# Up projection with both parts of x side by side as one 512-column operand, in 43 groups

## The chip, the cores and the metric

One core of a Trainium2 chip. The metric is the device time of one execution in microseconds (us). The program runs as five instruction streams: TensorE (PE, whose weight loads the profile lists as PEld), VectorE (DVE), ScalarE (ACT), GpSimd (POOL) and SyncE (SP), which issues the loads of the weights. They meet only through semaphores, and each works its queue in order.

## What is computed

Two transformer layers on 256 tokens of width 2048, in float32. The first is neighbourhood attention with a context, then a feed-forward network with a short convolution; the second is a hybrid of mLSTM and latent attention. What the change touches, cut to its core:

```python
x = x + g1 * y                                     # y: attention @ w_o
hf = modulate(rms_norm(x, norm_ffn_g), sh2, sc2)
gate, up = split(dwconv3(hf @ w_up, conv_w, conv_b), 2, axis=-1)   # w_up: 2048 x 11008
x = x + g2 * ((silu(gate) * up) @ w_down)          # w_down: 5504 x 2048
h = rms_norm_2(x, norm_g); proj = h @ w_in         # start of the second layer
```

`dwconv3` runs over the tokens with three taps for each column.

## The kernel before, in words

**Split product.** Each float32 operand is split in a high part (rounded to the form that PE streams fast) and a low part (the rest). A product is three matmuls: high by high, high of the weights by low of x, low of the weights by high of x (`product`, L903 to L905 where the weights are stationary, L894 to L896 where x is). Weights come from HBM in tiles of 128 x 1024 into 5 `raw` buffers (SP, L730); ACT writes the high part `wh` (L1129), DVE the low part `wl` (L1494), 3 buffers of each. ACT may write one when PE has finished the tile three before it. PE waits for `lo` at the first step of a tile.

**Order.** `products()` lists the products, `Program` makes one step for each chunk k of 128 rows of a product, and `schedule()` hangs pieces of other work onto steps by hand: `P.put(where, plus, job, key, phase, uses)` puts a phase `plus` steps behind the step `where`. Every engine walks the same list of steps and does its own part of each piece, in that order; `uses` counts the PSUM banks (`PS`, 4 in turn) that a piece takes. Idle steps (`tail`, `tail2`) stand where the residual must be complete. `weave` sets 32 tiles of `w_ada` among the weight tiles of the first up pass; they are summed up by DVE (L1480) and come with the same SP queue.

**Up projection.** `w_up` has 43 column blocks of 128 for the gate and 43 for the up half. Group g takes two of each (the last, g = 21, one of each), 16 steps of k. For each block x^T (`FHL`, 256 tokens) streams past the weights, so each matmul has 256 columns. The four results fill two banks of `PG[t % 2]`, t being the number of the product; the product after next may start when they are free. `up_out` empties them: ACT makes the middle tap with the bias (`CA`, L1233), DVE adds the outer taps straight out of PSUM (L1698, L1701), ACT applies silu (`CE`, L1241), POOL multiplies (L775), ACT writes the high part and DVE the low part of `HID` (L1248, L1709). Two passes: groups 0 to 10, then the first half of the down projection (`down0`, x stationary, 512 columns of weights moving), groups 11 to 21, then `down1`.

**Norm.** `residual` adds the gated result to `XT` (L1687 to L1691), ACT sums the squares (L1156), `norm` on DVE computes the inverse root by three Newton steps on 128x2 values (L1503 to L1522) and copies it to `xr` (L1603). `scale` writes x times `xr` (ACT L1162 for one half of the tokens, DVE L1607 for the other), `turned` transposes two chunks of 128 columns at a time on PE (L1053) and splits them (ACT L1438, DVE L1924, L1927; in the second layer L1444, L1933). Four of the eight pairs stand in the idle step, ahead of the first step of the next product; the rest behind steps 0, 2, 4 and 5.

**Attention start.** For the heads of groups 0 and 1 the inverse roots of q (`q_out`) and k (`k_sum`) run on DVE, `k_mul` spreads them through a matmul with DIAG (L912), and `attn` has ten phases per head: scores (0), bias, scale, maximum, exp, weighing (5), transposes (6), product with v (8).

## Time and profile before

| | us |
|---|---|
| three runs, median (lowest, highest) | 2614.59 (2613.82, 2615.66) |
| the profiled execution | 2615.56 |
| its span | 2613.7 |
| PE busy | 2548.9 |
| DVE busy | 1556.8 |
| ACT busy | 1211.7 |
| POOL busy | 109.8 |

The span is the time from the first to the last instruction in the profile. Busy time adds up the instructions of an engine; matmuls overlap, so their listed durations are longer than the distance from one start to the next, and the pace is read from the starts. The granted clock is the share of 2.4 GHz that PE was given: 1.00 is 2.4 GHz and 0.50 is 1.2 GHz. A wait is idle time of an engine, put down to the instruction that released it.

### The profile page before, as it was taken

The page shows a single profiled execution, that of the slowest core. Times are in us where ns is not written, and L with a number is a line of the kernel's source. Part 1 is how long each engine was busy: PE and PEld are TensorE (multiplying, and loading weights), DVE is VectorE, ACT ScalarE, POOL GpSimd, SP SyncE. Part 2 cuts the span into 40 slices and gives each one's busy share as a digit, 9 for nine tenths or more (in the row PEclk, how much of TensorE's full clock was granted, in tenths as well). Part 3 has the DMA queues.
Part 4 walks back from the last instruction along what each step waited for, and adds up shares of the span by engine and source line. Part 5 has one row for each costly group of instructions (what it writes and reads, how often), then busy time and mean ns, then how long its engine had stood idle before and what let it go on. Part 6 is the DMA issues. An engine that isn't in the chain of part 4 may idle for free.

```text
span 2613.7 us, 37292 instructions
## 1 busy us (share of the span) xinstructions
PE 2548.9 (98%) x15120; PEld 2223.9 (85%) x15120; DVE 1556.8 (60%) x2331; ACT 1211.7 (46%) x1788; POOL 109.8 (4%) x127
## 2 busy tenths in 40 slices
PE   5999999999989999999999989999999999999999
PEld 2678998888779999889998879988888888888887
DVE  3456666676567886556655566665555554545554
ACT  2333333333455444344554456555566665544443
POOL 1001000000000000000000000000000000000000
PEclk9999999999999999999999999999999999999999
DMA  9956566566457886655555655555555555555554
GB/s 335 355 195 194 188 198 197 189 218 197 161 164 247 264 261 210 194 188 185 184 181 186 197 149 172 170 162 185 174 167 156 163 163 179 183 193 183 188 186 168
DMA packets 377195, 511.61 MB, mean 196 GB/s; under 512 B 36771, under 2 KB 245762, under 8 KB 376512
## 3 DMA queue, kind: packets, MB, share of 16 engines
q1 hardware_dynamic: 374016, 501.11, 60.0%
q0 software_dynamic: 2864, 8.11, 1.0%
q8 instruction: 119, 1.95, 0.3%
q14 instruction: 52, 0.43, 0.1%
q10 hardware_dynamic: 144, 0.02, 0.0%
HBM read 506.93 MB, written 2.22 MB: 195 GB/s over the span
## 4 chain that ended last, share of the span: by engine, by line
PE 91%; ACT 3%; DVE 2%; SPq 2%; DMA 1%; issue 1%; DVEq 0%; ACTq 0%
PE PG L894 17%; PE PG L896 17%; PE PG L895 17%; PE PG L903 10%; PE PG L905 10%; PE PG L904 10%; SPq L730 1%; PE PS L994 1%; PE PS L978 1%; ACT wh L1129 1%; PE PS L1053 1%; DMA raw<-in_w_qkv 1%; PE PS L985 1%; PE PS L912 1%; PE PG L836 1%
## 5 line engine op out<-in xcount | busy, mean ns | idle before, releaser
L1494 DVE TENSOR_TENSOR wl<-raw,wh 128x1024 fp32r<-128x1024 f32 (+1 forms) x745 | 915.3, 1232 | 856.3 <-ACT wh L1129 854.6
L1129 ACT ACTIVATE wh<-raw 128x1024 fp32r<-128x1024 f32 (+1 forms) x745 | 786.2, 1057 | 1014.6 <-PE PG L896 664.0
L903 PE MATMUL PG<-FHL,wh 128*128 128x256 f32 x1376 | 391.2, 284 | 0.0
L905 PE MATMUL PG<-FHL,wl 128*128 128x256 f32 x1376 | 389.9, 283 | 0.0
L904 PE MATMUL PG<-FHL,wh 128*128 128x256 f32 x1376 | 389.9, 283 | 0.0
L894 PE MATMUL PG<-wh,HHL 128*128 128x512 f32 x832 | 331.1, 398 | 0.0
L896 PE MATMUL PG<-wl,HHL 128*128 128x512 f32 x832 | 324.8, 390 | 0.0
L895 PE MATMUL PG<-wh,HHL 128*128 128x512 f32 x832 | 324.1, 390 | 0.0
L903 PEld LDWEIGHTS PG<-FHL,wh 128*128 128x128 f32 x1376 | 264.7, 192 | 0.5 <-issue 0.5
L904 PEld LDWEIGHTS PG<-FHL,wh 128*128 128x128 f32 x1376 | 264.7, 192 | 0.5 <-issue 0.5
L905 PEld LDWEIGHTS PG<-FHL,wl 128*128 128x128 f32 x1376 | 264.7, 192 | 0.0
L896 PEld LDWEIGHTS PG<-wl,HHL 128*128 128x128 f32 x832 | 156.2, 188 | 33.6
L895 PEld LDWEIGHTS PG<-wh,HHL 128*128 128x128 f32 x832 | 156.5, 188 | 30.7
L894 PEld LDWEIGHTS PG<-wh,HHL 128*128 128x128 f32 x832 | 156.4, 188 | 30.3
L1480 DVE SCALAR_TENSOR_TENSOR ada_acc<-raw,CSs,ada_acc 128x1024 f32<-128x1024 f32 x120 | 160.5, 1337 | 1.9
L894 PE MATMUL PG<-wh,XHL 128*128 128x256 f32 x512 | 154.8, 302 | 0.0
L895 PE MATMUL PG<-wh,XHL 128*128 128x256 f32 x512 | 145.1, 283 | 0.0
L896 PE MATMUL PG<-wl,XHL 128*128 128x256 f32 x512 | 145.0, 283 | 0.0
L903 PE MATMUL PG<-XHL,wh 128*128 128x512 f32 (+1 forms) x384 | 137.2, 357 | 0.0
L894 PE MATMUL PG<-wh,HID 128*128 128x512 f32 x344 | 133.9, 389 | 0.0
L895 PE MATMUL PG<-wh,HID 128*128 128x512 f32 x344 | 133.9, 389 | 0.0
L896 PE MATMUL PG<-wl,HID 128*128 128x512 f32 x344 | 133.8, 389 | 0.0
(376 smaller groups left out, 4339.5 us busy)
## 6 DMA issues: line engine op xcount, KB each, us to landing
raw<-in_w_in SPq DMA_DIRECT2D x208, 512.0 KB, 3.4
raw<-in_w_up SPq DMA_DIRECT2D x344, 256.0 KB, 3.1
raw<-in_w_ada SPq DMA_DIRECT2D x128, 512.0 KB, 4.7
raw<-in_w_down SPq DMA_DIRECT2D x84, 512.0 KB, 4.5
raw<-in_w_qkv SPq DMA_DIRECT2D x80, 512.0 KB, 4.8
first<-in_w_ada SPq DMA_DIRECT2D x78, 256.0 KB, 7.1
raw<-in_w_o SPq DMA_DIRECT2D x32, 512.0 KB, 4.1
raw<-in_w_in SPq DMA_DIRECT2D x64, 256.0 KB, 3.0
```

What stands on the lines that cost most here:

```text
L730: sp.dma_start(dst[:, :, col:col + wd], src).then_inc(s_raw[P.slot[i]], 16)
L836: pe.matmul(dst, hi[:, cols], XHL[:, 0, k, 0:t], start=k == 0 and (j < 4 or j % 2 == 0), stop=False, skip_group_check=True)
L894: pe.matmul(dst, xh[:, cols], hi, start=step.first and j % per == 0, stop=False, skip_group_check=True)
L895: pe.matmul(dst, xl[:, cols], hi, start=False, stop=False, skip_group_check=True)
L896: end = pe.matmul(dst, xh[:, cols], lo, start=False, stop=step.last, skip_group_check=True)
L903: pe.matmul(dst, hi[:, c0:c1], xh, start=step.first and j % per == 0, stop=False, skip_group_check=True)
L904: pe.matmul(dst, hi[:, c0:c1], xl, start=False, stop=False, skip_group_check=True)
L905: end = pe.matmul(dst, lo[:, c0:c1], xh, start=False, stop=step.last, skip_group_check=True)
L912: pe.matmul(bank(u)[:, 0:128 * n], ones[:, :], flat(DIAG[:, 0:n, :]), start=True, stop=True).then_inc(S["side"], 1)
L1129: ac.activation(wh[n % NSPL][:, 0:src.shape[1]], src, ACT.Copy).then_inc(S["hi"], 1)
L1480: dv.scalar_tensor_tensor(out=acc[:, :], in0=raw_of(i), scalar=CSs[:, 0, k:k + 1], in1=acc[:, :], op0=ALU.mult, op1=ALU.add).then_inc(S["a ...
L1494: dv.tensor_tensor(wl[n % NSPL][:, 0:x], src, wh[n % NSPL][:, 0:x], ALU.subtract).then_inc(S["lo"], 1)
```

## The change

- **Operand.** `FHL` is laid out with the high and the low part of a chunk next to each other (k, part, token). A block is now one matmul of 512 columns (high weights by both parts) and one of 256 (low weights by the high part), added onto the first half.
- **Groups.** The results of a block fill a whole bank, so a group is one gate and one up block, 43 groups, in passes of 22 and 21. Group 0 computes group 1 with it, into both `PG`; product 1 has no steps of its own. Tiles of the other groups have 4 chunks of k and two segments of 128 columns, in rows of 512 bytes.
- **Emptying.** ACT copies the first halves of both banks into `UP`, DVE adds the second halves, which frees the banks; centre, taps, silu, product and split then work from SBUF on 256 columns. New semaphores `u_hi` and `conv`. The phases stand at steps 0, 1, 2, 3, 4, 7, 10 and 12 of the next group, three later for group 1. PE waits for both `PG` at the start of group 0.
- **Norm chain.** The sums of three of the four parts of the squares are made ahead (`presum`), `norm` finishes with one operation, there is no copy to `xr`. `warm`: 28 matmuls of 512 columns on weights already there, written to a `PG` that the next product overwrites, first in the idle step. The first pair of chunks takes two banks and is split chunk by chunk. Three pairs instead of four stand in the idle step, the rest behind steps 0, 2, 4, 6 and 8. In both norms.
- **Places.** `q_out` of group 1 goes from v 0 to v 1; `k_mul` of group 0 one step later; `attn` of groups 0 and 1 later; the residual of `down0` one step later; `rope` to other steps.

```diff
-UP_PASS = ((0, 11, 0, 22), (11, 22, 22, 21))
+UP_PASS = ((0, 22, 0, 22), (22, 43, 22, 21))
...
-            w = 256 if g < 21 else 128
-            add("up", g, "w_up", [(256 * g, w), (5504 + 256 * g, w)])
+            if g == 0:
+                add("up", g, "w_up", [(0, 256), (5504, 256)])
+            else:
+                add("up", g, "w_up", [(128 * g, 128), (5504 + 128 * g, 128)], 0, KC if g > 1 else 0)
...
-            P.put(("v", 0, 0), 1, "q_out", g, 1, 1)
-            P.put(("v", 0, 0), 2, "q_out", g, 2)
+            P.put(("v", g, 0), 1, "q_out", g, 1, 1)
+            P.put(("v", g, 0), 2, "q_out", g, 2)
...
-            P.put(("v", g, 0), 8 + 6 * j, "k_mul", (g, j), 0, 1)
-            P.put(("v", g, 0), 8 + 6 * j + 1, "k_mul", (g, j), 1)
+            late = 1 if g == 0 else 0
+            P.put(("v", g, 0), 8 + 6 * j + late, "k_mul", (g, j), 0, 1)
+            P.put(("v", g, 0), 9 + 6 * j + late, "k_mul", (g, j), 1)
...
-            plus = ((1, 2, 3, 4, 6, 7, 11, 12, 13, 14), (15, 16, 17, 18, 19, 20, 24, 25, 26, 27))
+            plus = ((2, 3, 4, 5, 6, 7, 15, 16, 18, 19), (20, 21, 22, 23, 24, 25, 32, 33, 34, 35))
         if g == 1:
-            plus = ((13, 14, 15, 16, 18, 19, 23, 24, 25, 26), (28, 29, 30, 31, 33, 34, 38, 39, 40, 41))
+            plus = ((21, 22, 23, 24, 25, 26, 31, 32, 33, 34), (35, 36, 37, 38, 39, 40, 45, 46, 47, 48))
...
+                if g == 2:
+                    P.put(at, n + 3, "presum", norm, 0)
...
+        P.put(at, 0, "warm", z, 0)
         P.put(at, 0, "norm", z, 0)
         for i in range(3):
             P.put(at, 0, "scale", (z, i), 0)
-        for i, n in enumerate((-1, -1, -1, -1, 0, 2, 4, 5)):
+        for i, n in enumerate((-1, -1, -1, 0, 2, 4, 6, 8)):
             where, plus = (at, 0) if n < 0 else (nxt, n)
-            P.put(where, plus, "turned", ("x" + z, i), 0, 1)
+            P.put(where, plus, "turned", ("x" + z, i), 0, 2 if i == 0 else 1)
...
-    for g in range(22):
-        nxt = ("down0", 0, 0) if g == 10 else ("down1", 0, 0) if g == 21 else ("up", g + 1, 0)
-        P.put(nxt, 1, "up_out", g, 0)
-        for i in range(4 if g < 21 else 2):
-            P.put(nxt, 2 + i, "up_out", g, 1 + i)
-        for phase, n in ((5, 6), (6, 8), (7, 10)):
-            P.put(nxt, n, "up_out", g, phase)
-    residual("down0", ("up", 11, 0), 0, None)
+    for g in range(43):
+        nxt = ("down0", 0, 0) if g == 21 else ("down1", 0, 0) if g == 42 else ("up", max(g + 1, 2), 0)
+        for phase, n in enumerate((0, 1, 2, 3, 4, 7, 10, 12)):
+            P.put(nxt, n + 3 * (g == 1), "up_out", g, phase)
+    residual("down0", ("up", 22, 0), 1, None)
...
+                if (name, g) == ("up", 0):
+                    w.wait_ge(S[f"out{(t + 1) % 2}"], (t + 1) // 2)
...
+            if name == "up":
+
+                for j in range(hi.shape[1] // 128):
+                    cols = slice(128 * j, 128 * j + 128)
+                    dst = PG[(t + j % 2) % 2][:, j // 2, :] if g == 0 else ps[:, j, :]
+                    pe.matmul(dst, hi[:, cols], flat(FHL[:, step.k, :, :]), start=step.first, stop=False, skip_group_check=True)
+                    end = pe.matmul(dst[:, 0:T], lo[:, cols], xh, start=False, stop=step.last, skip_group_check=True)
+            elif name in TOKENS:
...
+            elif job == "warm":
+
+                p = P.of["up" if key == "f" else "lat", 0]
+                t = p + 1
+                m = P.tile0[p]
+                w.wait_ge(S["lo"], m + 1)
+                w.wait_ge(S[f"out{t % 2}"], t // 2)
+                for n in range(28):
+                    pe.matmul(PG[t % 2][:, 0, :], wh[m % NSPL][:, 0:128], wh[m % NSPL][:, 0:512], start=True, stop=True)
...
+                    w.wait_ge(S["conv"], g - 1)
+                w.wait_ge(*product_done("up", g))
+                ac.activation(UP[b][:, :, :], result("up", g)[:, :, 0:T], ACT.Copy).then_inc(S["u_hi"], 1)
+            elif (job, phase) == ("up_out", 2):
...
+                if name in ("xf", "xh") and i == 0:
+                    if name == "xf":
+                        w.wait_ge(S["gain"], NCH + 1)
+                    for k in range(2):
+                        w.wait_ge(*full(u + k))
+                        end = ac.activation(dst[:, 0, k, :], bank(u + k)[:, 0:T], ACT.Identity, scale=gain[:, k:k + 1],
+                                            bias=MOD[:, 3, k:k + 1] if name == "xf" else 0.0)
+                        if k == 0:
+                            end.then_inc(S["xlo"], 1)
...
-                w.wait_ge(S["xsq"], 4 * nth("norm", key, 0))
-                dv.tensor_reduce(xss[:, :], xsq[:, :, :], AX, ALU.add).then_inc(c.sem, c.up())
-                y = rsqrt(xss[:, :], 2, EPS, mean=D)
-                dv.tensor_copy(xr[:, :], y).then_inc(S["xr"], 1)
+                n = nth("norm", key, 0)
+                w.wait_ge(S["xsq"], 4 * n)
+                w.wait_ge(c.sem, c.n)
+                dv.scalar_tensor_tensor(out=xss[:, :], in0=xsq[:, :, 3], scalar=1.0 / D, in1=xss[:, :], op0=ALU.mult,
+                                        op1=ALU.add).then_inc(c.sem, c.up())
+                rsqrt(xss[:, :], 2, 0.0, to=(xr[:, :], S["xr"], n))
+            elif job == "presum":
+                w.wait_ge(S["xsq"], 4 * P.order["norm", key, 0] + 3)
+                dv.tensor_reduce(xss[:, :], xsq[:, :, 0:3], AX, ALU.add).then_inc(c.sem, c.up())
+                w.wait_ge(c.sem, c.n)
+                dv.tensor_scalar(xss[:, :], xss[:, :], 1.0 / D, EPS, ALU.mult, ALU.add).then_inc(c.sem, c.up())
...
+            elif (job, phase) == ("up_out", 1):
                 g, b = key, key % 2
-                blocks = up_group(g)[1]
-                blk, z, j, ch = blocks[phase - 1]
-                dst = CA[b][:, z, T * j:T * j + T]
+                w.wait_ge(S["u_hi"], g + 1)
+                dv.tensor_tensor(UP[b][:, :, :], result("up", g)[:, :, T:2 * T], UP[b][:, :, :],
+                                 ALU.add).then_inc(out_sem("up", g), 1)
```

## Rows read from the trace of the kernel before

**Rows 1.** The page, part 1: busy time of each engine.
```profile
PE 2548.9 (98%) x15120; PEld 2223.9 (85%) x15120; DVE 1556.8 (60%) x2331; ACT 1211.7 (46%) x1788; POOL 109.8 (4%) x127
```

**Rows 2.** The page, part 5: first product line; its two sisters are alike.
```profile
L903 PE MATMUL PG<-FHL,wh 128*128 128x256 f32 x1376 | 391.2, 284 | 0.0
```

**Rows 3.** Time line (start, duration, what), PE, up projection.
```profile
800.18 0.28 PE L903 MATMUL PG<-FHL,wh 128*128 128x256 f32 x1
...
800.30 0.28 PE L904 MATMUL PG<-FHL,wh 128*128 128x256 f32 x1
```

**Rows 4.** Time line, PE, second down pass.
```profile
1503.03 0.39 PE L896 MATMUL PG<-wl,HID 128*128 128x512 f32 x1
1503.25 0.39 PE L894 MATMUL PG<-wh,HID 128*128 128x512 f32 x1
```

**Rows 5.** Who waited for whom, PE, 160:260 (total, times, longest).
```profile
PE PS L985 <- DVE SB L1671: 4.6, 1, 4.6
PE PS L912 <- DVE DIAG L1533: 2.1, 1, 2.1
```

**Rows 6.** Time line, end of wo to first up matmul.
```profile
757.23 0.39 PE L896 MATMUL PG<-wl,OHL 128*128 128x512 f32 x1
...
757.65 0.69 DVE L1687 TENSOR_TENSOR RTMP<-PG,G 128x512 f32<-128x512 f32 x1 [0.34 <-PE PG L896]
...
763.78 1.31 ACT L1162 ACTIVATE HNF<-XT,xr 128x256 f32<-128x256 f32 x3 [2.88 <-DVE xr L1603]
...
769.39 0.56 PE L903 MATMUL PG<-FHL,wh 128*128 128x256 f32 x1
```

**Rows 7.** Time line, end of down1 to first lat matmul.
```profile
1505.07 0.39 PE L896 MATMUL PG<-wl,HID 128*128 128x512 f32 x1
...
1512.48 1.31 ACT L1162 ACTIVATE HNH<-XT,xr 128x256 f32<-128x256 f32 x3 [2.81 <-DVE xr L1603]
...
1516.71 0.47 PE L894 MATMUL PG<-wh,HHL 128*128 128x512 f32 x1
```

**Rows 8.** Stretches; granted clock stands behind POOL, then DMA share, GB/s.
```profile
178.33:181.74 3.41, 3.41 (x11) 2.38 (x12) 3.41 (x3) 0.00 (x0) 1.10 (x1) 0.50 0.76 245
...
762.00:772.25 10.25, 6.42 (x29) 6.06 (x30) 6.85 (x21) 8.05 (x19) 0.00 (x0) 0.50 0.14 57
1509.50:1516.35 6.85, 2.87 (x13) 2.50 (x14) 4.45 (x21) 3.64 (x11) 0.00 (x0) 0.50 0.00 0
```

**Rows 9.** Time line, PE, at two changes of width.
```profile
247.28 0.40 PE L903 MATMUL PG<-XHL,wh 128*128 128x512 f32 x1
247.51 0.40 PE L904 MATMUL PG<-XHL,wh 128*128 128x512 f32 x1
...
276.20 0.28 PE L894 MATMUL PG<-wh,XHL 128*128 128x256 f32 x1
276.32 0.28 PE L895 MATMUL PG<-wh,XHL 128*128 128x256 f32 x1
```

**Rows 10.** Groups by form, 775:1000, DVE, then ACT (mean ns | idle before).
```profile
L1494 DVE TENSOR_TENSOR wl<-raw,wh 128x1024 fp32r<-128x1024 f32 x77 | 95.6, 1246 | 38.5 <-ACT wh L1129 38.2
L1480 DVE SCALAR_TENSOR_TENSOR ada_acc<-raw,CSs,ada_acc 128x1024 f32<-128x1024 f32 x30 | 42.5, 1416 | 0.0
...
L1129 ACT ACTIVATE wh<-raw 128x1024 fp32r<-128x1024 f32 x78 | 82.5, 1060 | 84.1 <-PE PG L905 82.0 <-DMA raw<-in_w_up 2.0
L1233 ACT ACTIVATE CA<-PG,fcb,fcw 128x256 f32<-128x256 f32 x36 | 17.2, 557 | 0.0
```

**Rows 11.** Stretches of the first and second up pass.
```profile
775.00:1000.00 225.00, 225.00 (x1868) 224.04 (x1867) 182.31 (x226) 114.91 (x145) 13.45 (x9) 1.00 0.80 254
1143.00:1390.00 247.00, 247.00 (x2037) 245.95 (x2036) 145.33 (x179) 119.73 (x145) 14.42 (x10) 1.00 0.58 183
```

**Rows 12.** DMA queues, 1365.9:1372.3, last up group (512-byte rows).
```profile
q1 hardware_dynamic: 2344, 1.17, 64.3%
```

**Rows 13.** Time line, DVE, end of the second q chain.
```profile
172.88 0.17 DVE L1633 COPY RQ<-CV 128x4 f32<-128x4 f32 x1
```

More of the change, by code:

```diff
@@ L535, in build @@
     fcb = at("fcb", [128, 86], F32, 153.25)
-    CA = [at(f"CA{i}", [128, 2, 512], F32, 154 + 4 * i) for i in range(2)]
-    CE = [at(f"CE{i}", [128, 512], F32, 162 + 2 * i) for i in range(2)]
+    CA = [at(f"CA{i}", [128, 2, T], F32, 154 + 2 * i) for i in range(2)]
+    UP = [at(f"UP{i}", [128, 2, T], F32, 158 + 2 * i) for i in range(2)]
+    CE = [at(f"CE{i}", [128, T], F32, 162 + i) for i in range(2)]
     HHL = at("HHL", [128, 2, KC, T], F32R, 76)
@@ L582, in build, with xready @@
     pad_dram = nc.dram_tensor("pad_rpb", [16 * 15 * 128 + 256], F32)
+    def xready(z, k):
+        u = use("turned", ("x" + z, k // 2), 0)
+        return emptied(u + k) if k < 2 else emptied(u)
     def bank(u):
@@ L770, in gpsimd @@
         po.dma_start(fcb[:, :], I["ffn_cb"]).then_inc(S["convw"], 16)
-        for g in range(22):
-            nb, _ = up_group(g)
-            b, n = g % 2, T * nb
+        for g in range(43):
+            b = g % 2
             w.wait_ge(S["gated_f"], g + 1)
-            po.tensor_tensor(CE[b][:, 0:n], CE[b][:, 0:n], CA[b][:, 1, 0:n], ALU.mult).then_inc(S["glu"], 1)
+            po.tensor_tensor(CE[b][:, :], CE[b][:, :], CA[b][:, 1, :], ALU.mult).then_inc(S["glu"], 1)
         w.wait_ge(*product_done("small", 0))
@@ L875, in operands @@
                 return VHL[:, 0, k, :], VHL[:, 1, k, :]
-            w.wait_ge(*emptied(use("turned", ("xh", k // 2), 0)))
+            w.wait_ge(*xready("h", k))
             return HHL[:, 0, k, :], HHL[:, 1, k, :]
@@ L1049, in piece @@
                 w.wait_ge(*free(u))
+                apart = name in ("xf", "xh") and i == 0
                 for ch in range(2):
+                    if apart and ch:
+                        end.then_inc(S["side"], 1)
+                        w.wait_ge(*free(u + 1))
+                    v, o = (u + ch, 0) if apart else (u, T * ch)
                     for n in range(2):
                         c0 = 128 * (2 * i + ch)
-                        end = pe.transpose(ps[:, T * ch + 128 * n:T * ch + 128 * n + 128], src[:, n, c0:c0 + 128],
-                                           ident[:, :])
+                        end = pe.transpose(bank(v)[:, o + 128 * n:o + 128 * n + 128], src[:, n, c0:c0 + 128], ident[:, :])
                 end.then_inc(S["side"], 1)
@@ L1514, in rsqrt @@
                              ALU.add).then_inc(c.sem, c.up())
-            for _ in range(3):
+            for i in range(3):
                 w.wait_ge(c.sem, c.n)
@@ L1521, in rsqrt @@
                 w.wait_ge(c.sem, c.n)
+                if i == 2 and to is not None:
+                    dv.scalar_tensor_tensor(out=to[0], in0=a, scalar=1.5, in1=y, op0=ALU.add,
+                                            op1=ALU.mult).then_inc(to[1], 1)
+                    w.wait_ge(*to[1:])
+                    return to[0]
                 dv.scalar_tensor_tensor(out=y, in0=a, scalar=1.5, in1=y, op0=ALU.add,
@@ L1697, in piece @@
                 w.wait_ge(S["centre"], g + 1)
-                dv.scalar_tensor_tensor(out=dst[:, 1:T], in0=up_view(g, blk)[:, 0:T - 1], scalar=fcw[:, ch, 0:1],
-                                        in1=dst[:, 1:T], op0=ALU.mult, op1=ALU.add).then_inc(c.sem, c.up())
+                w.wait_ge(*out_done("up", g))
+                dv.scalar_tensor_tensor(out=dst[:, 1:T], in0=u[:, 0:T - 1], scalar=fcw[:, ch, 0:1], in1=dst[:, 1:T],
+                                        op0=ALU.mult, op1=ALU.add).then_inc(c.sem, c.up())
@@ L1700, in piece @@
                 w.wait_ge(c.sem, c.n)
-                end = dv.scalar_tensor_tensor(out=dst[:, 0:T - 1], in0=up_view(g, blk)[:, 1:T], scalar=fcw[:, ch, 2:3],
+                end = dv.scalar_tensor_tensor(out=dst[:, 0:T - 1], in0=u[:, 1:T], scalar=fcw[:, ch, 2:3],
                                               in1=dst[:, 0:T - 1], op0=ALU.mult, op1=ALU.add)
-                if phase == len(blocks):
-                    end.then_inc(out_sem("up", g), 1)
+                if z == 1:
+                    end.then_inc(S["conv"], 1)
@@ L1920, in piece @@
                 _, dst, _, gain = turns[name]
+                if name in ("xf", "xh") and i == 0:
+                    for k in range(2):
+                        w.wait_ge(*((S["xlo"], 1 if name == "xf" else 2) if k == 0 else (S[name + "_hi"], 1)))
+                        if name == "xf":
+                            dv.tensor_scalar(MTF[0][:, k, :], bank(u + k)[:, 0:T], gain[:, k:k + 1], MOD[:, 3, k:k + 1],
+                                             ALU.mult, ALU.add).then_inc(c.sem, c.up())
+                            w.wait_ge(c.sem, c.n)
+                            end = dv.tensor_tensor(dst[:, 1, k, :], MTF[0][:, k, :], dst[:, 0, k, :], ALU.subtract)
+                        else:
+                            end = dv.scalar_tensor_tensor(out=dst[:, 1, k, :], in0=bank(u + k)[:, 0:T], scalar=gain[:, k:k + 1],
+                                                          in1=dst[:, 0, k, :], op0=ALU.mult, op1=ALU.subtract)
+                        end.then_inc(emptying(u + k), 1)
+                    return
                 w.wait_ge(S[name + "_hi"], i + 1)
```

67 lines of the change are left out of this document (31 added, 36 removed).

## The prediction

> **What bounds the kernel now.** I read the busy line and the chain on the page first, then the time line of TensorE (PE), then who waited for whom. PE is busy for 98% of the span [rows 1], so a change pays only if it shortens what PE streams, closes one of the few gaps in its time line, or keeps its clock up. The up projection is 86 blocks of 128 columns by 16 steps of k, 1376 blocks, and each of the three product lines has exactly that count [rows 2]. In it a 256-column matmul starts every 0.120 us [rows 3]; a 512-column one of the down projection every 0.227 us [rows 4]. The straight line through the two is 0.107 us per 256 columns plus 0.013 us per instruction, whatever its width. Four gaps matter: 2.1 us and 4.6 us at the first heads of the attention [rows 5], and the two stretches in which the residual is normalised, 757 to 769 us and 1505 to 1517 us [rows 6, 7]. After or in each of them the granted clock reads 0.50, the 1.2 GHz level, for a while [rows 8].
>
> **A. Fewer instructions in the up projection.** Now a block is three matmuls of 256 columns, 3 x 0.120 = 0.360 us. After it is one of 512 and one of 256 columns: the same 768 columns with one instruction fewer, 0.227 + 0.120 = 0.347 us. 1376 x 0.013 = 17.9 us off PE's stream, all on the path. The alternation of the two widths is nowhere in the trace in a long run. The rows at a change of width bracket it: behind narrow ones the first wide one takes 0.23, behind wide ones the first narrow one 0.12 [rows 9]; to the nanosecond, which the rows round, the first wide one takes 0.234 and the first narrow one 0.113. Taken apart these give a block of 0.340 to 0.354 us, so 8 to 27 us; their sum, 0.347, is the value I take, since an alternation has as many changes of one kind as of the other.
>
> The Trainium skill, page "TensorE: Matmul & The Clock Gate", section "Wait — 56ns, not 53.3ns?", gives a fixed cost of about 2.5 ns per warm matmul. By that figure one instruction fewer per block would be worth only 1376 x 2.5 ns = 3.4 us. The rows show 13 ns, and the measurement decides.
>
> **B. What the new layout costs the other engines.** A group now holds 2 blocks for 16 k, 11.1 us instead of 23.0 us of PE. Per group ACT copies 128x512 out of PSUM (between the 0.56 us of 256 columns and the 1.06 us of 1024 [rows 10], near 0.7 us), DVE adds the other halves (nearest row 0.69 us for 128x512 with PSUM [rows 6]), and silu, product, copy and subtraction run on 256 instead of 512 columns. In the first pass DVE gets 22 x 0.69 + 22 x 0.42 - 11 x 0.69 = 17 us more (0.42 us is my estimate of a 256-column pass from the slope of the 1024 and 512 column rows); its share there, 182.3 of 225 us [rows 11], rises from 0.81 to about 0.88. It stays below PE, so only bursts matter. Walk through a group boundary at time 0 (PE ends a group): ACT writes the high part of the tile after next until 1.1, copies until 1.8; DVE subtracts until 2.4, adds until 3.1, which frees the PSUM bank long before its next use at 11.1; ACT computes the two centres (0.56 each) until 4.2; DVE convolves one half until 5.2; the next high part ends at 5.3 and its low part at 6.5. PE wants it at 3 tiles x 2.78 = 8.3. With one w_ada pass in front (1.4 us, [rows 10]) it is ready at 7.8, and then a late DMA of 0.5 us is enough to be seen. In the second pass there is no w_ada and 1.8 us are left: nothing there. ACT has already waited 2.0 us for a raw tile in the first pass [rows 10], so I take 2 us of stalls, with 0 and 12 us as bounds (about 20 groups of up to 0.6 us).
>
> The weight tiles of groups 2 to 42 land in rows of 512 bytes instead of 1024. The one group that already does so shows 64.3% DMA share at 1.17 MB in 6.4 us, 183 GB/s [rows 12], against 0.58 at 183 GB/s in the same pass [rows 11], a tenth more. On 0.80 in the first pass that is 0.88: hidden, but it eats the same margin. A negative cost is excluded, since no work is removed from either.
>
> **C. Start of the up projection.** Last matmul of the output projection 757.23, xr ready 763.78, first up matmul 769.39 [rows 6]. The norm chain (operations 0.20 us apart) loses the reduction of four parts and the copy, and the scaling and the sum become one: about 0.5 us, xr at 763.3. After xr, ACT and DVE now finish the first pair of chunks and scale a fourth before PE, which has the fourth set of transposes ahead of the product, may begin. New: three scales on ACT (1.31 us) until 764.6, hi of k=0 (0.56) until 765.2, two DVE passes of 256 columns (0.42 to 0.56 each) until 766.2. The first matmul starts 3.2 us earlier. The 28 warm-up matmuls take 28 x 0.227 = 6.4 us, end at 763.8 and the transposes can't start before 763.9: hidden, and PE doesn't go idle, so the 0.50 stretch up to 772.25 [rows 8] should not be there. 2.9 us of it lie behind 769.39 and cost half: 1.4 us. Together 4.6 us gained. The transposes are spread further and ACT's queue (2.2 us per pair of chunks plus 1.06 us per tile, against 2.8 us of PE) is then just in time; what it loses there is in the bounds, 0 to 2 us.
>
> Against that, groups 0 and 1 now end together. Group 2 writes the banks of group 0, so PE waits by the walk above until the add at 3.1 us. That is a new stall that nothing covers. A gap of 2.3 us at 176 us was followed by a stretch at 0.50 of 3.4 us [rows 5, 8], so I add 1.7 us for the clock. Net of C: 4.6 - 3.1 - 1.7 = -0.2, nothing.
>
> **D. Start of the second layer.** The same norm chain without the shift, last and first matmul and scales: 1505.07, 1516.71 and 1512.48 [rows 7]. Norm 0.5 us shorter; after xr at 1512.0 three scales (1.3), hi and lo (0.5 each) put the first matmul at 1514.4: 2.3 us gained. The 28 warm-up matmuls end at 1511.7, before the transposes. The low clock there ended before the first matmul, so it gives no more.
>
> **E. Attention start.** The 2.1 us wait is for DIAG, which DVE writes after two q chains and the k chain. The second q chain (13 small operations, 3.0 us up to the copy at 172.88 [rows 13]) moves to v 1, and the spread is one step (12 x 0.120 = 1.44 us) later: the stall (2.3 us) and the half-speed stretch behind it (3.4 us, worth 1.7) go. In v 1 the chain finds the head's reduction moved behind it, so the next spread stays about in time. The 4.6 us wait is for the weighed scores of the second head. Its transposes now stand 12 steps behind the scores instead of 9, some 2.9 us later, while DVE (weights, w_ada, softmax) needs about as long as before; of 4.7 us I expect 1 left, and the clock stretch of 1.7 us gone. Sum of E: 2.3 + 1.7 + 3.7 + 1.7 = 9.4, bounds 4 and 10.
>
> **Moved, with no price.** The residual of the first down pass moves by one of 22 steps of 1.4 us, the rope pieces by a few; each stays under PE's stream. No queue of SP or POOL changes order; POOL's product runs in halves inside 11.1 us. If DVE had no slack they would cost their 2.6 us once.
>
> **Sum.** 17.9 (A) - 2 (B) + 0 - 0.2 (C) + 2.3 (D) + 9.4 (E) = 27.4 us. The profiled run took 2615.56 us (span 2613.7), 1.0 above the median of 2614.59: 2588 from the one, 2587 from the other. I say 2588.
>
> **Rivals.**
> 1. Bursts in the first pass. Low parts come late at most group boundaries where w_ada and a late DMA meet. 20 groups x 0.6 us = 12 us: 2598 to 2600. For it: DVE 0.88 and DMA 0.88 together; against it: nominal margin of 0.5 us even with w_ada in front. Chance 0.17.
> 2. The attention gaps only move, because DVE has as much to do between scores and transposes. E gives 2 instead of 9.4: 2595. Chance 0.13.
> 3. The wide instruction keeps what it seems to save: every change from narrow to wide costs the 0.234 and none gives the 0.113 back, so a block takes 0.354 and A gives 8 instead of 17.9: 2598, and nearer to 2602 if the 13 ns are hardly an instruction's own. The straight line through two widths speaks against it. Chance 0.06. The page named under A, with its 2.5 ns, belongs to this case.
> 4. Slower: the group boundary as a bottleneck. ACT copy, DVE add, ACT centre and DVE convolution follow one another, and the next tile's parts queue behind them, at all 41 boundaries. It decides from 27.4 / 41 = 0.67 us per boundary, that is if the low part is ready at 9.0 instead of 6.5 to 7.8. At 1.0 us it gives 2588 + 41 = 2629. The second pass's DVE share of 145.3 in 247 us [rows 11] speaks against it. Chance 0.05.
> 5. The clock and the release stall come out better (no stretch at 0.50, the stall inside one), or A lies towards 0.340: 2577 to 2584. Chance 0.09.
> Forecast: 0.50.
>
> The range 2577 to 2602 leaves out rival 4, the end of 3 and the tail of 5. A measurement of this kernel can tell about 0.2%, 5.2 us; all cases but 4 and a joint failure of A and E lie below 2609.4: faster 0.93, same 0.03, slower 0.04.
>
> **What would show it.** Up matmuls in turn 0.23 and 0.12 apart, with 1376 of each line; 11.1 us per group. A wait of PE of about 3 us for the DVE add at the start of group 2 (near 792 us) and no other above 1 us in the up projection. Clock 1.00 in both norm stretches, the first product matmul 9.0 instead of 12.2 us behind the last of the stage before, and 9.3 instead of 11.6 us in the second layer. No wait for DIAG, under 2 us for the scores. Wrong it would be if PE waits for low parts at each boundary, or if the pair takes 0.354 us.

## Result, and the profile after

The changed kernel takes 2623.22 us (median of six runs, 2621.86 to 2626.05), the kernel before 2614.20 in the same series: 1.0035 times as long, 95% interval 1.0022 to 1.0048. That is slower by some 9 us, where 27 us faster was forecast.

From the page of the changed kernel: span, busy line, and the two groups of matmuls of the up projection (line, operation, count, busy time and mean ns of one, idle time before).

```profile
span 2622.1 us, 34913 instructions
PE 2554.9 (97%) x13800; PEld 2158.4 (82%) x13800; DVE 1582.2 (60%) x2397; ACT 1232.0 (47%) x1872; POOL 111.3 (4%) x148
...
L899 PE MATMUL PG<-FHL,wh 128*128 128x512 f32 x1376 | 495.0, 404 | 23.8 <-DVE wl L1533 18.4
L900 PE MATMUL PG<-FHL,wl 128*128 128x256 f32 x1376 | 388.1, 282 | 0.0
```

There are 1376 instructions fewer, as planned, but 23.8 us of PE's idle time now stand ahead of the wide ones. They answer to [rows 2], where three lines had 1376 each.

The time line of PE gives the milestones. First the two norm stretches: last matmul of the stage before, end of the norm chain (`xr`), first product matmul.

```profile
747.41 0.39 PE L908 MATMUL PG<-wl,OHL 128*128 128x512 f32 x1
...
753.38 0.16 DVE L1562 SCALAR_TENSOR_TENSOR xr<-CV 128x2 f32<-128x2 f32 x1
...
756.52 0.47 PE L899 MATMUL PG<-FHL,wh 128*128 128x512 f32 x1 [0.85 <-DVE FHL L1981]
...
1515.22 0.39 PE L908 MATMUL PG<-wl,HID 128*128 128x512 f32 x1
...
1522.03 0.16 DVE L1562 SCALAR_TENSOR_TENSOR xr<-CV 128x2 f32<-128x2 f32 x1
...
1524.47 0.50 PE L906 MATMUL PG<-wh,HHL 128*128 128x512 f32 x1
```

The up projection starts 9.11 us behind the output projection instead of 12.16 [rows 6], the second layer 9.25 instead of 11.64 [rows 7]. And the output projection ends at 747.41 instead of 757.23. Now the two up passes, as windows from first to last matmul: length, busy time (and instructions) of PE, PEld, DVE, ACT, POOL, then granted clock, DMA share and GB/s. The three short ones are the stretches at the low clock in the first pass.

```profile
756.50:1044.00 287.50, 264.51 (x1436) 223.37 (x1437) 217.69 (x295) 146.40 (x221) 15.95 (x21) 0.98 0.72 216
1163.70:1401.00 237.30, 237.30 (x1344) 205.79 (x1343) 159.24 (x207) 128.81 (x184) 14.79 (x20) 1.00 0.64 185
784.87:791.70 6.83, 6.06 (x19) 5.22 (x20) 1.59 (x4) 2.08 (x4) 0.00 (x0) 0.51 0.52 155
842.90:846.31 3.41, 3.41 (x11) 2.86 (x12) 3.41 (x4) 1.22 (x2) 0.00 (x0) 0.51 0.77 220
866.79:870.20 3.41, 3.41 (x13) 2.92 (x12) 1.92 (x3) 2.62 (x4) 0.73 (x1) 0.51 0.54 155
```

The same first pass in the kernel before:

```profile
769.00:1029.00 260.00, 260.00 (x2138) 258.08 (x2137) 205.17 (x257) 133.58 (x173) 14.93 (x10) 0.99 0.76 241
```

There PE was busy throughout; now 23.0 us of 287.5 are idle. The second pass has none. So the account, from start to start, in us against before:

| stretch | before | after | difference |
|---|---|---|---|
| up to the last matmul of the output projection | 757.23 | 747.41 | -9.8 |
| to the first up matmul | 12.16 | 9.11 | -3.05 |
| first up pass | 259.9 | 287.5 | **+27.6** |
| first down pass | 119.7 | 119.7 | 0 |
| second up pass | 241.9 | 237.4 | -4.5 |
| second down pass | 114.1 | 114.1 | 0 |
| to the first matmul of the second layer | 11.6 | 9.25 | -2.4 |
| the rest | | | +0.5 |

The sum is 8.3, next to the difference of the spans (2622.1 - 2613.7 = 8.4). The starts went nearly as forecast, and the second up pass gained 4.5 us of the 8.7 that 672 blocks at 0.013 us were to give; what turned the result is the first up pass. The first row of the table is one trace against one: up to that point eleven further kernels run the same code as the changed one, and in their traces the same matmul starts between 746.7 and 749.9 us, so that this gain reads 7.4 to 10.5 us. Who let PE wait, from 740 to 1050 us (total, times, longest):

```profile
PE PG L899 <- DVE wl L1533: 18.4, 19, 2.0
PE PG L899 <- DVE UP L1746: 4.4, 1, 4.4
PE PG L899 <- DVE FHL L1981: 0.9, 1, 0.9
```

Nineteen times PE waits up to 2 us for a low part of the weights (`wl`), and once for the addition that frees the banks. One such wait in the time line, with a few rows of PE:

```profile
890.09 1.22 DVE L1533 TENSOR_TENSOR wl<-raw,wh 128x1024 fp32r<-128x1024 f32 x1
891.23 1.28 DVE L1519 SCALAR_TENSOR_TENSOR ada_acc<-raw,CSs,ada_acc 128x1024 f32<-128x1024 f32 x1
...
892.42 0.48 DVE L1753 SCALAR_TENSOR_TENSOR CA<-UP,fcw,CA 128x255 f32<-128x255 f32 x1
892.94 0.48 DVE L1756 SCALAR_TENSOR_TENSOR CA<-UP,fcw,CA 128x255 f32<-128x255 f32 x1
893.52 0.42 ACT L1273 ACTIVATE CE<-CA 128x256 f32<-128x256 f32 x1 [3.46 <-DVE CA L1756]
893.84 1.04 ACT L1154 ACTIVATE wh<-raw 128x1024 fp32r<-128x1024 f32 x1
...
894.18 0.28 PE L900 MATMUL PG<-FHL,wl 128*128 128x256 f32 x1
894.91 2.48 DVE L1533 TENSOR_TENSOR wl<-raw,wh 128x1024 fp32r<-128x1024 f32 x2 [1.49 <-ACT wh L1154]
896.19 0.50 PE L899 MATMUL PG<-FHL,wh 128*128 128x512 f32 x1 [1.74 <-DVE wl L1533]
```

No engine is full here: ACT stands idle for 3.46 us ahead of silu, DVE for 1.49 us ahead of the low part. It is a chain through both. Step 4 of the group has DVE do the low part of a tile, then the `w_ada` pass (1.28 us) that follows it in the plan, and only then the second half of the taps. Silu on ACT waits for the taps. The high part of the next tile stands behind silu in ACT's queue, and its low part follows that. PE is out of tiles at 894.3 and goes on at 896.19. With groups half as long this order comes twice as often, and each has only four tiles in which to recover.

### The profile page after: what moved, and what is told of

It is laid out like the page before. It is cut to its first block, busy times and chain, and to the rows that moved or that the text cites. A ratio compares the mean times of both kernels' runs of the same rounds, so it can differ in the third digit from the quotient of the medians.

```text
span 2622.1 us, 34913 instructions
## 1 busy us (share of the span) xinstructions
PE 2554.9 (97%) x13800; PEld 2158.4 (82%) x13800; DVE 1582.2 (60%) x2397; ACT 1232.0 (47%) x1872; POOL 111.3 (4%) x148
## 4 chain that ended last, share of the span: by engine, by line
PE 84%; DVE 6%; ACT 4%; issue 2%; DMA 2%; SPq 1%; DVEq 0%; ACTq 0%
PE PG L906 17%; PE PG L908 17%; PE PG L907 17%; PE PG L899 8%; PE PG L900 4%; PE PG L915 4%; PE PG L917 4%; PE PG L916 4%; ACT wh L1154 2%; DVE wl L1533 2%; SPq L734 1%; DVE ada_acc L1519 1%; PE PS L1015 1%; PE PS L999 1%; PE PS L1079 1%
## 5 line engine op out<-in xcount | busy, mean ns | idle before, releaser
L899 PE MATMUL PG<-FHL,wh 128*128 128x512 f32 x1376 | 495.0, 404 | 23.8 <-DVE wl L1533 18.4
L899 PEld LDWEIGHTS PG<-FHL,wh 128*128 128x128 f32 x1376 | 261.2, 190 | 94.9 <-DVE wl L1533 25.6
L900 PEld LDWEIGHTS PG<-FHL,wl 128*128 128x128 f32 x1376 | 262.6, 191 | 0.5 <-issue 0.5
L915 PE MATMUL PG<-XHL,wh 128*128 128x512 f32 (+1 forms) x384 | 137.0, 357 | 0.0
L917 PE MATMUL PG<-XHL,wl 128*128 128x512 f32 (+1 forms) x384 | 129.4, 337 | 0.0
L916 PE MATMUL PG<-XHL,wh 128*128 128x512 f32 (+1 forms) x384 | 129.2, 336 | 0.0
```

The costliest lines, as they stand in the source:

```text
L899: pe.matmul(dst, hi[:, cols], flat(FHL[:, step.k, :, :]), start=step.first, stop=False, skip_group_check=True)
L900: end = pe.matmul(dst[:, 0:T], lo[:, cols], xh, start=False, stop=step.last, skip_group_check=True)
L915: pe.matmul(dst, hi[:, c0:c1], xh, start=step.first and j % per == 0, stop=False, skip_group_check=True)
L916: pe.matmul(dst, hi[:, c0:c1], xl, start=False, stop=False, skip_group_check=True)
L917: end = pe.matmul(dst, lo[:, c0:c1], xh, start=False, stop=step.last, skip_group_check=True)
```

## Experiments

**Theories.** T1, order: the `w_ada` pass in front of the taps delays silu and with it the next tile. T2, load: DVE simply has too much in the first pass. T3, transfers: 512-byte rows make tiles late. T4, ACT alone: silu's place is the fault. T5, pace: whatever the stalls, the alternation of the widths takes most of what a block should save.

**All of the change except the up projection's new form.** The norm chains, the warm-up, the places of the attention, `FHL` and groups as before.

> The kernel before with everything of the change except the up projection: attention places, norm chain, warm-up matmuls, finer first transposes. The traces put the attention at -9.8 us, the start of the up projection at -3.1 and the start of the second layer at -2.4, and the clock in the first group adds up to 1.4. If the parts add, this runs at 2614.6 - 15.3 to 16.7, so 2598 to 2600 us, with no wait of PE over 1 us in the up passes, and the change's own part, the new up projection, costs +24 us. If the parts interact (the loss in the up pass comes from the new places of the transposes or of the residual), the first up pass is longer than 260 us here too and the time is above 2605.

Measured: 2599.42 us, 0.994 of before (0.9923 to 0.9956). From the page's windows and the waits of 740 to 1050 us:

```profile
756.10:1015.20 259.10, 259.06 (x2140) 257.14 (x2141) 206.64 (x260) 134.94 (x176) 14.93 (x10) 1.00 0.76 242
...
PE PG L913 <- DVE FHL L1971: 0.8, 1, 0.8
```

The other parts of the change bring 16 us (2615.6, before in the same series, to 2599.4), and the new form of the up projection alone costs 24 us (25 if each kernel is set against the kernel before in its own series). In the old form PE waits for nothing in this pass but 0.8 us at its start. So the parts add, as expected, and the loss is not one of the other changes in themselves.

**Two wide, then two narrow matmuls in each step.**

```diff
-for j in blocks: wide(j); narrow(j)
+for j in blocks: wide(j)
+for j in blocks: narrow(j)
```

> The changed kernel with the two wide matmuls of a step first and the two narrow ones behind them, instead of in turn: half the changes of width. In the change a pair takes 0.2353 + 0.1170 = 0.352 us. If the changes of width cost it, one step of two pairs takes 0.234 + 0.227 + 0.113 + 0.120 = 0.694 us or 0.347 per pair, the second up pass shrinks from 237.3 to about 234 us and the kernel by 3 to 7 us. If the pair costs 0.352 whatever the order (what the wide matmul streams is the limit), nothing moves: 2623. The waits in the first pass stay in both cases.

Measured: 2620.02 us, 1.0015 (1.0006 to 1.0025). The second pass is 3.4 us shorter (234.1 instead of 237.4), as expected: a pair takes 0.348 instead of 0.353 us, so the changes of width do cost something, and T5 holds for about half of what a block should save. The first pass isn't shorter (288.0): PE waits 20.5 instead of 18.4 us for low parts. A faster PE only waits longer here.

**The `w_ada` passes of DVE shortened to 8 of 1024 columns in the first up pass.** Their loads stay; the sums over `w_ada` are incomplete, so a part of the modulation isn't computed.

> The changed kernel; in the first up pass DVE adds only 8 of the 1024 columns of each w_ada tile (left out: most of the gate of the down projection), the loads are unchanged. If the stalls come from the order on DVE and ACT (w_ada pass ahead of the taps, taps ahead of silu, silu ahead of the next high part), nearly all waits of PE for low parts go, and the first up pass falls from 287.5 to about 265 us: 2600 to 2603. If they come from the weight loads in rows of 512 bytes, the waits stay: 2620 or more.

Measured: 2599.07 us, 0.9938 (0.9918 to 0.9957); waits for low parts 3.6 us (6 times), first pass 261.7. So the passes are what makes the low parts late. The transfers were all still there, though their buffers come free earlier, so this alone doesn't rule them out; but in the changed kernel ACT waited for a load only once in this pass, 0.2 us. The run doesn't tell T1 from T2.

**Weight tiles as one segment of 256 columns.** Rows of 1024 bytes again; the columns taken aren't those of the reference, so another product of the same shape is computed.

> The changed kernel; the weight tiles of groups 2 to 42 come as one segment of 256 columns, rows of 1024 bytes, instead of two of 128 (the values are other columns of w_up: left out is the right choice of columns). Order theory: the waits stay, 2620 to 2624, since ACT waited only 0.2 us for loads. Load theory: the waits go, 2600.

Measured: 2623.34 us, 1.003 (1.0018 to 1.0042), 20.2 us of waits (20). T3 falls.

**Silu and what follows one step later.** Phases at steps 0, 1, 2, 3, 4, 8, 11, 12, so that the high part of the tile at step 8 is ahead of silu.

```diff
-for phase, n in enumerate((0, 1, 2, 3, 4, 7, 10, 12)):
+for phase, n in enumerate((0, 1, 2, 3, 4, 8, 11, 12)):
```

> The changed kernel with silu at step 8 instead of 7 and the copy of the high part at 11 instead of 10 of the next group: on ACT both now stand behind the high part of the weight tile that opens at step 8. Order theory, with ACT's queue as the link that counts (silu waits for the taps, the taps for a w_ada pass, and the next high part stands behind silu): most of the 18.4 us of waits for low parts and half of the lost clock go, first up pass 287.5 down to about 270, 2605 to 2610 us. If the link that counts is on DVE alone (w_ada and taps straight ahead of the low part), less than 5 us come back: 2618 or more.

Measured: 2621.37 us, 1.0022 (1.0012 to 1.0032); 14.6 us of waits in 21 places, first pass 284.0. It is a miss: 270 was expected for the first pass, and under 5 us of gain was the mark of the rival, a cause on DVE alone. In one group the wait of 1.34 us (at 958.9 us in the changed kernel) becomes three, of 0.69, 0.20 and 0.17. Over the pass ACT waits 32.6 instead of 52.6 us ahead of silu, but now 24.8 us (0.3 before) for the product ahead of the copy to `HID`, and high parts stand behind that. The longest wait of all is now 3.4 us, from another chain (`rope`, shown with the last experiment but one). T4 falls as the whole cause.

**The same DVE work in another order.** The `w_ada` passes no longer follow the low part of a tile but the pieces of the step behind.

```diff
 if step.opens: split_upto(step.m + 2)        # low part; w_ada stays back
 for job in P.side[s]: piece(job)
+if step.k == 1 or step.k > 1 and step.opens: split_upto(-1)   # w_ada
```

> The changed kernel with the same w_ada passes on DVE in the up projection, but each behind the pieces of steps 1, 4, 8 and 12 instead of straight behind the low part: in the time in which DVE waits for ACT's centre, and behind the taps. The work of DVE is the same to the instruction. Order theory: the waits for low parts fall below 6 us, first up pass 265 to 270, 2602 to 2608 us. Load theory (DVE has too much to do in the first pass): nothing moves, 2620 or more.

Measured: 2607.39 us, 0.9967 (0.9954 to 0.998); first pass 270.5 instead of 287.5. The same place in a group, and the waits:

```profile
882.86 1.23 DVE L1535 TENSOR_TENSOR wl<-raw,wh 128x1024 fp32r<-128x1024 f32 x1
884.00 0.48 DVE L1755 SCALAR_TENSOR_TENSOR CA<-UP,fcw,CA 128x255 f32<-128x255 f32 x1
884.52 0.48 DVE L1758 SCALAR_TENSOR_TENSOR CA<-UP,fcw,CA 128x255 f32<-128x255 f32 x1
884.92 1.28 DVE L1519 SCALAR_TENSOR_TENSOR ada_acc<-raw,CSs,ada_acc 128x1024 f32<-128x1024 f32 x1
885.09 0.42 ACT L1273 ACTIVATE CE<-CA 128x256 f32<-128x256 f32 x1 [2.27 <-DVE CA L1758]
...
PE PG L899 <- DVE wl L1535: 7.7, 12, 2.2
PE PG L899 <- DVE UP L1748: 3.2, 1, 3.2
```

Silu starts 2.23 us behind the start of the low part instead of 3.43. ACT gains in two places, not one: it waits for the addition (L1265) 48.3 us in this pass instead of 61.1, and for the taps (L1273) 43.1 instead of 52.6. Not one operation was taken away, and 17 us of the pass are gone: the order of the `w_ada` passes is shown as the cause, and T2 falls as the main one. How much of it runs through silu, as T1 has it, and how much through the addition, isn't separated.

**All wide matmuls of a tile, then all narrow ones.** PE waits for the high part first, and for the low part only ahead of the narrow ones.

> The changed kernel; PE starts a weight tile when its high part is there, does the 8 wide matmuls of the tile and then the 8 narrow ones, and waits for the low part only before these. One change of width per 8 matmuls: the pair should take 0.348 us, second up pass 234 us or less. The low part may come half a tile, 1.4 us, later: waits of up to 2.0 us shrink by 1.4, so about 4 us are left of 18.4. Together 2598 to 2605 us. If a pair costs the same in any order, the second pass stays at 237.

Measured: 2619.83 us, 1.0017 (1.0006 to 1.0027), first pass 285.2: a miss. The time line in the second pass, then the waits of the first:

```profile
1200.11 2.00 PE L901 MATMUL PG<-FHL,wh 128*128 128x512 f32 x8
1201.95 1.12 PE L908 MATMUL PG<-FHL,wl 128*128 128x256 f32 x8
1202.90 0.86 PE L901 MATMUL PG<-FHL,wh 128*128 128x512 f32 x3
...
PE PG L901 <- ACT wh L1164: 18.7, 18, 2.1
```

A low part could now be 1.8 us later, but it never was the first late link: the high part is itself late, by as much. The pace did change. Eight wide ones take 1.84 us, eight narrow ones 0.95, so a pair takes 0.349 us instead of 0.353.

**All of it together.** Order of a tile, `w_ada` behind, silu later, and the copy and addition of group 0 in its own last step.

> All of it: tile order, w_ada behind, silu late, and the copy and the add of group 0 ahead of the next tile's parts (which lets group 2 start 1.5 instead of 4.6 us after group 0, without the stretch at clock 0.50). If each does what it should: both up passes at 0.348 us per pair with 2 to 3 us of waits, first pass 249, second 233 us: 2599.4 of the kernel with the old up projection, less 11 + 8, plus 2: about 2583 us. If the loss in the first pass is load and not order, about 2605.

Measured: 2596.30 us, 0.9925 (0.9909 to 0.9942), PE waiting 5.4 us for high parts and 1.5 for the banks. It is faster than both kernels. The first pass takes 262.6 us and missed its 249. Against the first experiment (2599.42) it is only 3 us better. The traces show why: the second pass takes 234.6 instead of 241.9 us, the first 262.6 instead of 259.1. Mended, the new form gives 7.3 us in one pass and still loses 3.5 in the other.

**One warm-up matmul instead of 28.**

> The changed kernel with 1 instead of 28 warm-up matmuls in each norm stretch; nothing is left out of the result. The gaps between the last matmul of the stage before and the first transposes stay at about 6.4 us, with PE idle. If the warm-up is what keeps the clock up, the transposes and the first matmuls of the up projection stand at a granted clock of 0.50, as before the change (762 to 772.25 us there, 2.9 us of it behind the first product matmul, worth 1.4 us): the first up pass is 1.5 to 3 us longer, the up start about 0.5 us later, and the same start delay in the second layer: 2623.2 + 2 to 5 = 2625 to 2628. Rival: the shorter gap alone (9.1 instead of 12.2 us) already spares the low clock: no stretch at 0.50 in either norm stretch and 2623, within 1 us of the changed kernel.

Measured: 2629.59 us, 1.0055 (1.004 to 1.007). The windows of the low clock near the two norm stretches, and PE's wait ahead of the transposes:

```profile
754.36:761.18 6.82, 4.65 (x19) 4.34 (x20) 5.36 (x19) 5.22 (x12) 0.00 (x0) 0.50 0.31 129
1525.77:1532.60 6.83, 5.14 (x18) 4.50 (x19) 5.23 (x18) 5.70 (x13) 0.00 (x0) 0.50 0.01 2
...
PE PS L1079 <- ACT HNF L1187: 6.1, 1, 6.1
```

Both stretches at 1.2 GHz are back, and the rival (a shorter gap is enough) falls. Of the 6.6 us at the end of the trace 2.4 arose ahead of the first norm stretch, where the warm-up plays no part. From there the start takes 0.1 us more, the first pass 2.2, the second start 0.8, and the stages behind it 1.2, together 4.3 us. About 1 us of the 2.2 comes from a stretch at the low clock at 901 us, behind a gap of 2.0 us; the changed kernel has the same gap (894.2 us) without a stretch, so whether that one hangs on the warm-up isn't shown. The warm-up is worth 3 to 4 us. The time itself lies 1.6 us above the 2625 to 2628 expected.

**`w_ada` behind and silu later, without the order of a tile.**

> The changed kernel with the w_ada passes of DVE behind the pieces (as in e6_ada_behind) and silu one step later (as in e5_silu_late), the order of the matmuls unchanged. Nothing is left out. If what remained of waits for low parts with the passes moved (7.7 us, 12 times) is the second link, silu standing ahead of the next high part on ACT, the waits fall to 3 us or less and the first up pass from 270.5 to about 264: 2607.4 - 6 = 2601, still 5 us behind the kernel with tile order (2596.3), since the pair stays at 0.353 instead of 0.349 us (1376 x 0.004 = 5.5). Rival: what remained comes from bursts of DVE that no place of silu changes: waits stay at 6 to 8 us and the time at 2605 to 2607.

Measured: 2605.22 us, 0.9963 (0.9949 to 0.9977); 7.5 us of waits (10) against 7.7 (12), first pass 269.4 against 270.5. The rival was right: silu's place is worth 1 us here, and the waits that remain have another origin. The longest is 2.2 us in both kernels. With `w_ada` behind alone, it looks like this:

```profile
828.07 0.26 ACT L1282 ACTIVATE CSN<-ang 128x64 f32<-128x64 f32 x1 [5.25 <-DVE ang L1808]
828.24 1.04 ACT L1154 ACTIVATE wh<-raw 128x1024 fp32r<-128x1024 f32 x1
...
829.31 1.22 DVE L1535 TENSOR_TENSOR wl<-raw,wh 128x1024 fp32r<-128x1024 f32 x1 [1.27 <-ACT wh L1154]
...
830.59 0.67 PE L899 MATMUL PG<-FHL,wh 128*128 128x512 f32 x1 [2.21 <-DVE wl L1535]
```

That is `rope`, which the change moved. DVE computes the angles in small operations from 825.53 to 828.04 us, ACT stands idle for 5.25 us until it can take their sine (`CSN`), and the high part of the next tile stands behind that in its queue. The same chain stands ahead of the wait of 1.9 us at 833.97 in the changed kernel, of the 3.4 us at 832.96 with silu late, and of the longest wait (2.8 us at 825.56) with everything together. In the kernel before and in the first experiment ACT waits 3.9 and 4.3 us at the two places where this chain stands, and PE not at all. Putting it elsewhere was not tried.

**Copy and addition of group 0 in its last step, alone.**

```diff
+if g == 0 and phase < 2: P.put(("up", 0, 15), 0, "up_out", g, phase); continue
```

> The changed kernel with ACT's copy and DVE's addition of group 0 at the last step of its own 16 instead of step 0 and 1 behind it, so ahead of the parts of the next tile. Nothing is left out. The wait of PE for the freed banks at the start of the third group (4.4 us) falls to the copy, the addition and the way between them: about 0.7 + 0.7 + 0.3 = 1.7 us; with it the stretch at a clock of 0.50 behind it (6.8 us, worth 3.4) shortens or goes: 2623.2 - 2.7 - 0 to 3.4 = 2617 to 2620.5. Rival: the wait is on the order of the queues in nothing, ACT and DVE have only the product's end to wait for, and what is won is given back by the next low part that now comes later: 2622 to 2624.

Measured: 2619.55 us, 1.0019 (1.001 to 1.0029), first pass 282.9 instead of 287.5.

```profile
PE PG L902 <- DVE wl L1536: 19.0, 19, 2.0
PE PG L902 <- DVE UP L1749: 1.5, 1, 1.5
```

The 4.4 us become 1.5 as computed, and the clock's stretch at 784.87 us is gone. Little is given back: the low parts cost 19.0 instead of 18.4 us.

| kernel | us | first pass | second pass | gaps of PE | at low clock |
|---|---|---|---|---|---|
| before | 2614.2 | 259.9 | 241.9 | 0.8 (2) | 1.4 |
| changed | 2623.2 | 287.5 | 237.4 | 27.1 (23) | 5.8 |
| all but the new form | 2599.4 | 259.1 | 241.9 | 0.8 (2) | 0.0 |
| two wide, two narrow | 2620.0 | 288.0 | 234.1 | 29.0 (23) | 5.0 |
| short `w_ada` | 2599.1 | 261.7 | 237.4 | 8.8 (9) | 1.5 |
| rows of 1024 bytes | 2623.3 | 286.6 | 237.4 | 29.0 (24) | 3.2 |
| silu later | 2621.4 | 284.0 | 237.4 | 23.0 (23) | 5.1 |
| `w_ada` behind | 2607.4 | 270.5 | 237.4 | 13.7 (15) | 3.1 |
| `w_ada` behind and silu later | 2605.2 | 269.4 | 237.4 | 12.9 (12) | 1.6 |
| copy first | 2619.6 | 282.9 | 237.4 | 24.5 (22) | 3.6 |
| order of a tile | 2619.8 | 285.2 | 234.6 | 26.5 (20) | 4.9 |
| all together | 2596.3 | 262.6 | 234.6 | 9.2 (10) | 2.0 |

The last two columns are worked out from the starts of PE's matmuls in the first pass: us lost in distances over 0.46 us, with their count, and in matmuls at the low clock, each against 0.236 us for a wide and 0.118 for a narrow one. A gap is some 0.2 us longer than the wait in the list, since PE's last matmul still counts as busy for a while. Which matmuls at the edge of a stretch are counted in shifts the last column by up to 0.5.

## Why the prediction was wrong

**A, the saving of a block: right in kind, too large.** The pace of the second pass of the changed kernel, from the time line:

```profile
1199.75 0.40 PE L899 MATMUL PG<-FHL,wh 128*128 128x512 f32 x1
1199.98 0.28 PE L900 MATMUL PG<-FHL,wl 128*128 128x256 f32 x1
...
1206.11 0.40 PE L899 MATMUL PG<-FHL,wh 128*128 128x512 f32 x1
```

18 pairs in 6.36 us are 0.353 us each, against 0.347 forecast and 0.354 in rival 3. The second pass gained 4.5 us. In the first, gaps (26.3 us more), the low clock (4.4 more) and other work (0.3 more) are 31.0 us by the last table's way of working, and the pass is 27.6 longer, so 3.4 us are left for its blocks. By the pace of the second pass (4.5 us for 672 blocks) its 704 blocks gave 4.7. The missing 1.3 us belong to the waits: the first wide matmul behind one takes some 0.34 instead of 0.236 us, and there are about 20. So the blocks gave 9.2 us together instead of 17.9. The step that failed is the choice of the sum of two straight paces, with the argument that an alternation has as many changes of one kind as of the other. It has, but they don't weigh the same: on average a wide one costs 0.236 us here (0.227 in a long run) and a narrow one 0.117 (0.120). The upper bracket, taken from the first matmul behind a change of width [rows 9], was the value to take. By the 2.5 ns of the Trainium skill, page "TensorE: Matmul & The Clock Gate", section "Wait — 56ns, not 53.3ns?", the estimate was 3.4 us; no run here agrees with it, and the saving measured lies between the two.

**B, stalls in the first pass: 25.9 instead of 2 us. This is the step that turned the result.** The gaps other than the one for the banks cost 27.1 - 4.5 - 0.8 = 21.8 us more than before, the stretches at the low clock behind them 2.8, and the slow first matmuls 1.3. My walk through the boundary of a group had the right pieces but two errors. It put one `w_ada` pass in front of the low part and found 0.5 us left. In the queue the pass stands behind the low part and ahead of the taps, where it delays not DVE's next tile but ACT, which waits for the addition and the taps; that moving the passes gave back 17 us shows it. And the walk ended at step 4, before the piece (step 7) that carries the delay over. The second error is that it counted the order of one engine at a time: busy shares of 0.76 for DVE and 0.51 for ACT (217.7 and 146.4 of 287.5 us) say nothing on a chain that goes from one to the other and back within four tiles. Rival 1 had the place (low parts, only in the first pass, `w_ada`) and about the count (20 times), but a size of 0.6 us instead of some 1.1. Rival 4 had the size of a boundary (1.0 us) and the chain of copy, addition, centre and taps, but at all 41 boundaries. The second pass, without `w_ada`, has none.

The low clock was left out of B altogether. Before the change a gap of 2.3 us was followed by such a stretch [rows 5, 8]; after it four gaps in the pass are 2.0 to 2.3 us long (from 831.8, 840.7, 864.0 and 894.2 us), and the second and third were followed by one (842.90 and 866.79 us).

**C, start of the up projection.** The start came 3.05 us earlier (3.2 forecast), with no low clock in it (1.4, right). The wait for the banks was 4.5 us instead of 3.1, and the stretch of 6.83 us at the low clock behind it cost 3.0 instead of 1.7. The time line shows the missing term:

```profile
781.39 1.06 ACT L1154 ACTIVATE wh<-raw 128x1024 fp32r<-128x1024 f32 x1 [1.71 <-PE PG L900]
...
782.35 0.58 ACT L1255 ACTIVATE UP<-PG 128x512 f32<-128x512 f32 x1
782.47 1.22 DVE L1533 TENSOR_TENSOR wl<-raw,wh 128x1024 fp32r<-128x1024 f32 x1 [1.54 <-ACT wh L1154]
783.62 1.28 DVE L1519 SCALAR_TENSOR_TENSOR ada_acc<-raw,CSs,ada_acc 128x1024 f32<-128x1024 f32 x1
784.81 0.68 DVE L1746 TENSOR_TENSOR UP<-PG,UP 128x512 f32<-128x512 f32 x1
785.64 0.77 PE L899 MATMUL PG<-FHL,wh 128*128 128x512 f32 x1 [4.35 <-DVE UP L1746]
```

It is the same `w_ada` pass: 1.2 us between the low part and the addition. With the passes behind, the wait for the banks fell from 4.4 to 3.2 us. C came to a loss of 3.1 us instead of 0.2.

**D, second layer.** 2.4 us gained, 2.3 forecast. That the clock gives no more was right for the changed kernel, but only thanks to the warm-up: without it the earlier start puts the first 2.7 us of the product into the stretch at 1.2 GHz.

**Moved, with no price.** The prediction put `rope` at nothing, since its operations stay under PE's stream. They do, but their last result goes through ACT, ahead of the next high part: 1.9 of the 18.4 us of waits stand behind it in the changed kernel. This is part of B.

**E, attention start.** 9.8 us by these two traces, 9.4 forecast. The wait for `DIAG` fell from 2.1 to 0.9 us, the one for the scores (4.6 us) is gone, and so are both stretches at the low clock [rows 5, 8]. Between 150 and 260 us one line is left in the list of waits:

```profile
PE PS L924 <- DVE DIAG L1577: 0.9, 1, 0.9
```

**The sum.** 9.2 - 25.9 - 3.1 + 2.4 + 9.8 = -7.6 us; with 0.3 of other work in the pass and 0.5 in the stages behind the second norm that is -8.4. The range ended at 2602 because I gave the bursts a size that just used up the margin, and left no room for a price of 1 us at 20 places; the chance of 0.05 for slower was far too small for a step whose own margin was 0.5 us.

**Left open.** With `w_ada` behind, 7.7 us of waits stay, and with everything together 5.4; neither silu's place nor the order of the matmuls takes them away. `rope` accounts for 2.2 and 2.8 of them; the others haven't been followed link by link. How the 17 us divide between the addition and silu is open too. Also open is why the first wide matmuls behind narrow ones are slower (below).

## What to carry to other kernels

Halving a group doubles how often the chain through PSUM copy, addition, activation and split must fit between two tiles: write out each engine's queue over the whole group, with every background pass in its actual place, and follow the chain from engine to engine, for busy shares don't show it. Put background work behind the pieces that another engine waits for; that alone was worth 17 us of a pass of 287.5 here, with no operation removed. The same holds for a short chain of small operations whose result ACT must take ahead of a split. And a gap of 2 us on PE can cost more than 2 us, through the clock.

## What was not expected of the hardware

- **A change of width costs.** In the second pass of the kernel with the order of a tile, the mean distances from one start to the next in a run of eight are, over the 84 tiles of the pass:

```
wide    0.234 0.236 0.229 0.232 0.231 0.227 0.227 0.226
narrow  0.114 0.119 0.120 0.119 0.121 0.120 0.120 0.119
```

  The first five wide ones cost 0.029 us above the steady pace in sum, the first narrow one gains 0.006. In strict alternation the steady pace is never reached.
- **A short pause can bring a longer stretch at the low clock.** Two of four gaps of 2.0 to 2.3 us were followed by 3.4 us at 1.2 GHz, the wait of 4.4 us by 6.8. 28 matmuls on data of no use, in a time in which PE would stand still for 6.1 us, kept the clock at 2.4 GHz; with the second norm stretch they were worth 3 to 4 us.
